# A third set for the accumulated weight sums in the up projection of a convolutional FFN, with the first sum's loads placed sooner and cache copies placed later

## The chip, the core and the metric

The kernel is one launch on one core of a Trainium2 chip. TensorE (PE) does the matrix products, VectorE (DVE) and ScalarE (ACT) elementwise work, GpSimd (POOL) small copies and those DMAs that add to what already stands at their destination, and SyncE (SP) issues most other DMAs. The metric is the device time in microseconds, median over runs.

## What is computed

One decoder layer over 512 prompt rows and 32 sample rows (8 sequences of 4 new tokens), all in float32: RMS norm, one input projection, retention and dilated attention, an output projection, and a feed-forward part with a causal convolution of width 3. The change lies in this last part and in the copying of the rolling key/value windows:

```python
def conv_ffn(h, conv_state, w_ffn_up, conv_w, conv_b, w_ffn_down):
    u = h @ w_ffn_up                       # (T, 1024) @ (1024, 2*2816)
    ext = jnp.concatenate([conv_state.astype(u.dtype), u], axis=1)
    c = conv_b + sum(conv_w[i] * ext[:, i:i + T] for i in range(CONV_W))
    g, val = c[..., :D_FF], c[..., D_FF:]
    f = (jax.nn.gelu(g, approximate=True) * val) @ w_ffn_down
    return f, ext[:, -(CONV_W - 1):]

# dilated_sample, for each of three groups of 128, 512 and 2048 cached rows:
new_buf = jnp.concatenate([buf, jnp.stack([k_new, v_new], axis=2)], axis=1)[:, -Wb:]
```

The new windows are the old ones moved by four rows, so almost all of each is a copy from one place in memory to another ("move" below, 511 KB for the large pieces). There are 88 moves: 44 are issued in the loop beside the input projections, 44 from the first up-projection loads on (iterator `moves`, L674).

## The kernel before

**Three passes for one product.** Every float32 product is done as three products of rounded halves: a weight tile is loaded raw, ACT makes its high part (a copy to fp32r), DVE the low part (raw minus high), and PE multiplies high by high, high by low and low by high.

**The up projection, in pairs.** The 5632 output columns are 22 pairs of tiles of 128 columns, a gate tile and a value tile (pair n, FT = 22). Pairs 0 to 2 (NPLAIN = 3) are plain: the two weight slots of a pair pass through `wraw`, `whi`, `wlo` (L2133, `up_half`). Pairs 3 to 21 are done by a scheme that needs seven half-size products instead of eight, on sums and differences of weight quarters and of operand quarters. Six of the seven are made in three passes (`three_passes`, L2185: 12 matmuls of 128 x 272), product 4 in one plain float32 pass (L2245, 8 matmul rows). PE's order is that of `up_products` (L87): for pair n products 6, 5, 7, then product 1 of pair n + 1, then 4 and 3 of pair n, then product 2 of pair n + 1 (L2256 to L2265). The semaphore `product` counts them; other engines and the queues wait for its values.

**The weight sums.** For pair n the tile `s13_raw` must hold the two quarters of the value weights' low half plus a quarter of the gate weights and of the value weights. It is filled in two steps: SP loads the value's low half twice side by side (`load_v_low`, L686, one DMA of 512 KB), and when that has landed POOL issues a DMA that adds 512 KB of gate and value weights to it in place (`add_to_v_low`, L959). Then ACT makes the high part (`sums_13_hi`, L1461), DVE adds `v_high` for the second sum (`sum_2`, L2844) and makes the low part over the raw tile (`sums_13_lo`, L2862, `s13_low` has the place of `s13_raw`). There are two sets of it, by n - 3 modulo 2 (`pair_set`). The tile of pair n is last read by product 7 of pair n, so SP issues the load for pair n + 2 after product 7 of pair n (L711).

**Queues of the engines.** Each engine works in program order. ACT does, in pair n: first_tap(n - 1), `keep_second(n)` (the result of product 6), **`sums_13_hi(n + 1)`**, `keep_third(n)` (the result of product 7, L1494), gelu(n - 1), `gate_hi(n + 2)` (L1451, high part of the gate weights of pair n + 2), `keep_first(n + 1)`, `sums_24_hi(n + 1)`, value_first(n), first_tap(n) (L1547 to L1570). Product 4 of pair n waits for `keep_third(n)` (r_neg, L2243), product 6 of pair n + 1 for the low part of the second sums (s24_lo, L2216). DVE's order is at L2927 to L2950. SP does in pair n: wait for product 2, `load_g(n + 2)`; wait for product 7, `load_v_low(n + 2)`, one move; wait for product 4, `load_v_high(n + 2)`, one move (L707 to L716). POOL does conv_heads(n + 2), add_to_v_low(n + 2), conv_tails(n).

**The first summed pair.** SP loads the last four plain slots with a move behind each (L695), and then those of pair 3 (L699 to L702). The set 1 tile of pair 4 lies over `whi`, so it can be loaded only when the plain pairs are done (w_used, L705).

**The down projection.** 22 slots of 512 KB through `wraw` (L722). SP puts one move behind each load until there are none left, which is the case after six. Near its end POOL reads back the residual rows (L987).

Of the kernel before, what the change touches and what calls it, by code (L numbers as in the profile page):

```python
# [44 lines left out]
TILES = 5  # L45
# [215 lines left out]
def build_layer(nc, a, o):  # L261
# [259 lines left out]
    g_in, vl_in, vh_in, sum_in = ([sem(f"{nm_}{e}") for e in range(2)] for nm_ in ("g_in", "vl_in", "vh_in", "sum_in"))  # L521
# [4 lines left out]
    x2_saved, x2_back = sem("x2_saved"), sem("x2_back")  # L526
# [61 lines left out]
    def set_count(n):  # L588

        return 16 * ((n - NPLAIN) // 2 + 1)  # L590

# [29 lines left out]
    def _(sp):  # L621
# [85 lines left out]
        for n in range(NPLAIN, FT - 2):  # L707
# [4 lines left out]
            load_v_low(n + 2)  # L712
            move(*next(moves))
# [33 lines left out]
    def _(pool):  # L747
# [182 lines left out]
        for p, i in enumerate(NORM_ORDER):  # L930
            pool.wait_ge(x2_ready, 2 * p + 2)
            pool.dma_start(x2_dram[i, 0:rows(i), :], xo[0:rows(i), i, :]).then_inc(x2_saved, 16)
# [52 lines left out]
        pool.dma_start(gfin[:], a["norm_ffn_post"].broadcast_to([128, D])).then_inc(gfin_in, 16)  # L985
        for i in range(TILES):
            pool.dma_start(xo[0:rows(i), i, :], x2_dram[i, 0:rows(i), :]).then_inc(x2_back, 16)  # L987
# [8 lines left out]
    def _(act):  # L996
# [7 lines left out]
        def w_split(s):  # L1004
# [456 lines left out]
        def sums_13_hi(n):  # L1461

            e = pair_set(n)
            act.wait_ge(sum_in[e], set_count(n))
# [4 lines left out]
            nc.scalar.activation(s13_high[e][:], s13_raw[e][:], ACT.Copy).then_inc(s13_hi, 1)  # L1469
# [122 lines left out]
    def _(pe):  # L1592
# [592 lines left out]
        def three_passes(b, fresh, Wh, Wl, w0, Th, Tl):  # L2185

            for k in range(4):
                cut = slice(w0 + 128 * k, w0 + 128 * k + 128)
                mm(b[:, 0:HALF], Wh[:, cut], Th(k), start=fresh and k == 0, stop=False, skip_group_check=not fresh)  # L2189
                mm(b[:, 0:HALF], Wh[:, cut], Tl(k), start=False, stop=False, skip_group_check=not fresh)  # L2190
                last = mm(b[:, 0:HALF], Wl[:, cut], Th(k), start=False, stop=k == 3, skip_group_check=not fresh)  # L2191
# [862 lines left out]
```

## Time and profile before

| | before |
|---|---|
| median of 3 runs (lowest to highest) | 1034.82 us (1033.66 to 1035.28) |
| profiled execution: time, span of its trace | 1034.72 us, 1032.9 us |
| PE busy (matmul) | 978.5 us, 95% |
| DVE, ACT, POOL busy | 600.7, 424.8, 230.7 us (58%, 41%, 22%) |
| DMA queue of SP, DMA queue of POOL | 130.76 MB, 63.07 MB |
| pair 3, product 4 starts; pair 20, product 4 starts | 649.20 us, 871.77 us |

The profile is one execution with the time of every instruction on each engine. The span begins with the first instruction; the profiled execution's own time is 1.8 us more than its span, and 0.1 us under the median of the three runs. PE is busy nearly all the time on average, but an average over the whole span hides the one stretch, the summed pairs from 635 to 885 us, in which it isn't. "idle ... <- X" behind a row means that the engine stood still before it, and that X ended the wait. A PE row's duration includes what it spends in the pipeline behind its neighbours, so the rate of PE is read from start to start.

### The profile page before, as it was taken

The page shows a single profiled execution, that of the slowest core. Times are in us where ns is not written, and L with a number is a line of the kernel's source. Part 1 is how long each engine was busy: PE and PEld are TensorE (multiplying, and loading weights), DVE is VectorE, ACT ScalarE, POOL GpSimd, SP SyncE. Part 2 cuts the span into 40 slices and gives each one's busy share as a digit, 9 for nine tenths or more (in the row PEclk, how much of TensorE's full clock was granted, in tenths as well). Part 3 has the DMA queues.
Part 4 walks back from the last instruction along what each step waited for, and adds up shares of the span by engine and source line. Part 5 has one row for each costly group of instructions (what it writes and reads, how often), then busy time and mean ns, then how long its engine had stood idle before and what let it go on. Part 6 is the DMA issues. An engine that isn't in the chain of part 4 may idle for free. (4 is left out here: it accounts for less than half of the span.)

```text
span 1032.9 us, 19094 instructions
## 1 busy us (share of the span) xinstructions
PE 978.5 (95%) x7470; PEld 858.5 (83%) x7470; DVE 600.7 (58%) x1029; ACT 424.8 (41%) x851; POOL 230.7 (22%) x394
## 2 busy tenths in 40 slices
PE   5999999999999999999999998889988899999997
PEld 4788778779999999998887797888988888777775
DVE  5255125534458876872165896677876677743135
ACT  5233232442453333322234654455554554633413
POOL 2102004134252434445010002222222221000200
PEclk9999999999999999999999999999999999999999
DMA  6644545547687676679453455777877776242723
GB/s 236 232 155 160 179 151 182 178 158 243 240 285 233 208 220 211 202 237 318 150 169 102 148 187 133 204 204 208 246 203 218 215 216 181 94 146 83 218 83 115
DMA packets 52070, 195.02 MB, mean 189 GB/s; under 512 B 7704, under 2 KB 8152, under 8 KB 50448
## 3 DMA queue, kind: packets, MB, share of 16 engines
q1 hardware_dynamic: 30784, 130.76, 37.2%
q0 software_dynamic: 21200, 63.07, 21.8%
q8 instruction: 59, 0.97, 0.4%
q14 instruction: 27, 0.22, 0.1%
HBM read 181.57 MB, written 56.27 MB: 230 GB/s over the span
## 5 line engine op out<-in xcount | busy, mean ns | idle before, releaser
L2309 DVE TENSOR_TENSOR wlo<-wraw,whi 128x1024 fp32r<-128x1024 f32 x94 | 114.9, 1222 | 265.1 <-ACT whi L1021 264.9
L1021 ACT ACTIVATE whi<-wraw 128x1024 fp32r<-128x1024 f32 x96 | 101.6, 1060 | 307.0 <-PE bank L1625 183.1
L1623 PE MATMUL bank<-whi,T1h 128*128 128x512 f32 (+1 forms) x288 | 114.5, 397 | 0.5 <-POOL wlo L762 0.3
L1705 PE MATMUL bank<-T1h,whi 128*128 128x272 f32 x384 | 113.4, 295 | 0.0
L1711 PE MATMUL bank<-T1h,wlo 128*128 128x272 f32 x384 | 111.0, 289 | 0.0
L1624 PE MATMUL bank<-wlo,T1h 128*128 128x512 f32 (+1 forms) x288 | 110.8, 385 | 0.0
L1625 PE MATMUL bank<-whi,T1l 128*128 128x512 f32 (+1 forms) x288 | 110.8, 385 | 0.0
L1710 PE MATMUL bank<-T1l,whi 128*128 128x272 f32 x384 | 110.4, 287 | 0.0
L1705 PEld LDWEIGHTS bank<-T1h,whi 128*128 128x128 f32 x384 | 72.3, 188 | 4.8 <-issue 4.5
L1710 PEld LDWEIGHTS bank<-T1l,whi 128*128 128x128 f32 x384 | 72.4, 189 | 0.0
L1711 PEld LDWEIGHTS bank<-T1h,wlo 128*128 128x128 f32 x384 | 72.2, 188 | 0.0
L1623 PE MATMUL bank<-whi,fTh 128*128 128x512 f32 x176 | 71.4, 406 | 0.0
L2245 PE MATMUL bank<-t4raw,v_high 128*128 128x272 f32 x152 | 45.5, 450 | 26.1 <-ACT rr L1498 26.1
L1624 PE MATMUL bank<-wlo,fTh 128*128 128x512 f32 x176 | 69.5, 395 | 0.0
L1623 PEld LDWEIGHTS bank<-whi,T1h 128*128 128x128 f32 x288 | 58.5, 203 | 13.1 <-issue 3.5
L1625 PE MATMUL bank<-whi,fTl 128*128 128x512 f32 x176 | 69.4, 394 | 0.0
L1625 PEld LDWEIGHTS bank<-whi,T1l 128*128 128x128 f32 x288 | 58.7, 204 | 10.0
L1624 PEld LDWEIGHTS bank<-wlo,T1h 128*128 128x128 f32 x288 | 58.8, 204 | 8.8
L2245 PEld LDWEIGHTS bank<-t4raw,v_high 128*128 128x128 f32 x152 | 31.2, 214 | 34.2 <-issue 28.0
L964 POOL DMA_DIRECT2D s_raw<-in_weights x19 | 22.7, 1196 | 121.0 <-DMA s_raw<-in_weights 113.6
L2494 DVE TENSOR_TENSOR prod<-kvk,qbc 128x512 f32<-128x512 f32 x48 | 33.0, 688 | 25.2 <-DMA qbc<-sample_queries 24.3
L1438 ACT ACTIVATE c<-u,convp 128x560 f32<-128x560 f32 x44 | 37.4, 856 | 20.3 <-DVE u L2888 19.6
(363 smaller groups left out, 2572.6 us busy)
## 6 DMA issues: line engine op xcount, KB each, us to landing
wraw<-in_weights SPq DMA_DIRECT2D x104, 512.0 KB, 4.4
out_s_kv_g<-in_cache_kv_g SPq DMA_DIRECT2D x64, 511.0 KB
qbc<-sample_queries POOLq DMA_DIRECT2D x48, 256.0 KB, 5.1
s_raw<-in_weights SPq DMA_DIRECT2D x19, 512.0 KB, 4.8
g_raw<-in_weights SPq DMA_DIRECT2D x19, 512.0 KB, 6.4
s_raw<-in_weights POOLq DMA_DIRECT2D x19, 512.0 KB, 7.2
kvk<-in_cache_kv_g POOLq DMA_DIRECT2D x32, 256.0 KB, 3.8
kvv<-in_cache_kv_g POOLq DMA_DIRECT2D x16, 512.0 KB, 8.2
```

Of the source, the lines that this page charges most:

```text
L964: pool.dma_start(s13_raw[e][:].rearrange("p (a c) -> p a c", a=2), src, accum_op=ALU.add).then_inc(sum_in[e], 16)
L1021: nc.scalar.activation(w_halves(s)[0], wraw[:, s % 2, :], ACT.Copy).then_inc(w_hi, 1)
L1438: nc.scalar.activation(cbs[:, n % 2, j, :], ubs[:, n % 3, j, 2:UW], ACT.Identity, scale=convp[:, tile, 2:3], bias=convp[:, tile, 3:4]).the ...
L1623: one = mm(P[i][:, 0:w], xh, Wh, start=st, stop=False)
L1624: mm(P[i][:, 0:w], xh, Wl, start=False, stop=False)
L1625: return one, mm(P[i][:, 0:w], xl, Wh, start=False, stop=sp_)
L1705: one = mm(dst, Wh, Th[:, k, c], start=k == 0, stop=False)
L1710: mm(dst, Wh, Tl[:, k, c], start=False, stop=False)
L1711: last = mm(dst, Wl, Th[:, k, c], start=False, stop=k == kt - 1)
L2245: last = mm(P[bank_a(n)][:, 0:HALF], v_high[e][:, 128 * k:128 * k + 128], t4raw[:, k, :], start=False, stop=k == 3, skip_group_check=True)
L2309: v.tensor_tensor(lo, wraw[:, s % 2, :], hi.bitcast(F), ALU.subtract).then_inc(w_lo, 1)
L2494: step(v.tensor_tensor(prod[:].rearrange("p (t n) -> p t n", t=2), keys, qbc[n % 3][:], ALU.mult))
```

## The change

It does five things.

1. A third set of `s13_raw`/`s13_low`, in columns of `T1h` that are no longer read once the plain pairs are done. The set of pair n is n - 3 modulo 3 (`sum_set`). Because the free columns are rows of 256 with gaps, the tile is now seen as 4 x 256 throughout. The high part keeps two sets.
2. SP now issues the low value half of pair n + 3 after product 7 of pair n, and POOL the adding DMA for pair n + 3. The load of pair 5 stands directly behind that of pair 4.
3. Each of the two DMAs is issued as two of 256 KB; a sum is complete after both.
4. The loads of pair 3 stand ahead of the last two plain slots and of the moves.
5. One move in each summed pair instead of two, and 25 moves instead of 6 in the down projection (one behind even slots, two behind odd ones). The read-back of the residual rows uses the same semaphore as their saving.

```diff
-    s13_raw = [sb(f"s13_raw{e}", S13_AT[e], [128, SLOT]) for e in range(2)]
-    s13_low = [sb(f"s13_low{e}", S13_AT[e], [128, SLOT], R) for e in range(2)]
-    s13_high = [sb(f"s13_high{e}", S13H_AT[e], [128, SLOT], R) for e in range(2)]
+    s13_raw = [sb(f"s13_raw{e}", S13_AT[e], [128, 4, 256]) for e in range(2)]
+    s13_low = [sb(f"s13_low{e}", S13_AT[e], [128, 4, 256], R) for e in range(2)]
+    s13_raw.append(sb("s13_raw2", 0, [128, 4, NTOK])[:, :, HALF:HALF + 256])
+    s13_low.append(sb("s13_low2", 0, [128, 4, NTOK], R)[:, :, HALF:HALF + 256])
+    s13_high = [sb(f"s13_high{e}", S13H_AT[e], [128, 4, 256], R) for e in range(2)]
...
+    def sum_set(n):
+        return (n - NPLAIN) % 3
+    def sum_count(n):
+        return 16 * ((n - NPLAIN) // 3 + 1)
...
         def load_v_low(n):
-            src = w_dram[S_UP + 2 * n + 1][:, 512:SLOT].unsqueeze(1).broadcast_to([128, 2, 512])
-            sp.dma_start(s13_raw[pair_set(n)][:].rearrange("p (a c) -> p a c", a=2), src).then_inc(vl_in[pair_set(n)], 16)
+            r = sum_set(n)
+            src = w_dram[S_UP + 2 * n + 1][:, 512:SLOT].rearrange("p (c w) -> p c w", c=2)
+            for a_ in range(2):
+                sp.dma_start(s13_raw[r][:, 2 * a_:2 * a_ + 2, :], src).then_inc(vl_in[r], 16)
...
-        for s in range(S_UP + 2, S_UP + 2 * NPLAIN):
+        for s in range(S_UP + 2, S_UP + 4):
             load_one(s)
-            move(*next(moves))
         sp.wait_ge(w_used, S_UP)
         load_v_low(NPLAIN)
+        load_v_high(NPLAIN)
         load_g(NPLAIN)
-        load_v_high(NPLAIN)
         load_v_high(NPLAIN + 1)
+        for s in range(S_UP + 4, S_UP + 2 * NPLAIN):
+            move(*next(moves))
+            load_one(s)
         sp.wait_ge(w_lo, S_UP + 2 * NPLAIN)
         load_g(NPLAIN + 1)
         sp.wait_ge(w_used, S_UP + 2 * NPLAIN)
         load_v_low(NPLAIN + 1)
+        load_v_low(NPLAIN + 2)
         for n in range(NPLAIN, FT - 2):
...
             sp.wait_ge(product, PRODUCT_NO[n, 7])
-            load_v_low(n + 2)
-            move(*next(moves))
+            if n + 3 < FT:
+                load_v_low(n + 3)
...
-            for m in itertools.islice(moves, 1):
+            for m in itertools.islice(moves, 2 if s % 2 else 1):
...
         def add_to_v_low(n):
-            e = pair_set(n)
-            pool.wait_ge(vl_in[e], set_count(n))
-            src = w_dram[S_UP + 2 * n:S_UP + 2 * n + 2].rearrange("s p (h c) -> p h s c", h=2)[:, 0]
-            pool.dma_start(s13_raw[e][:].rearrange("p (a c) -> p a c", a=2), src, accum_op=ALU.add).then_inc(sum_in[e], 16)
+            r = sum_set(n)
+            pool.wait_ge(vl_in[r], 2 * sum_count(n))
+            for a_ in range(2):
+                src = w_dram[S_UP + 2 * n + a_][:, 0:512].rearrange("p (c w) -> p c w", c=2)
+                pool.dma_start(s13_raw[r][:, 2 * a_:2 * a_ + 2, :], src, accum_op=ALU.add).then_inc(sum_in[r], 16)
...
+            if n == NPLAIN:
+                add_to_v_low(NPLAIN + 1)
+                add_to_v_low(NPLAIN + 2)
             if n >= 1 and n + 2 < FT:
                 conv_heads(n + 2)
-            if n == NPLAIN - 1:
-                add_to_v_low(NPLAIN + 1)
-            if NPLAIN <= n < FT - 2:
-                add_to_v_low(n + 2)
+            if NPLAIN <= n < FT - 3:
+                add_to_v_low(n + 3)
             conv_tails(n)
```

SP's queue around the first summed pairs, before. `wraw` are the last plain slots, `out_s_kv` a move, `s13_raw`, `g_raw` and `v_high` the loads of summed pairs (0 and 1 the set):

```order
L680 DMA wraw_52<-in_weights 128x1024
L654 DMA out_s_kv_g2<-in_cache_kv_g2 16x8176
L680 DMA wraw_52<-in_weights 128x1024
L654 DMA out_s_kv_g2<-in_cache_kv_g2 16x8176
L689 DMA s13_raw0_195<-in_weights 128x2x512
L684 DMA g_raw0_189<-in_weights 128x1024
L693 DMA v_high0_207<-in_weights 128x512
L693 DMA v_high1_208<-in_weights 128x512
L684 DMA g_raw1_190<-in_weights 128x1024
L689 DMA s13_raw1_196<-in_weights 128x2x512
L684 DMA g_raw0_189<-in_weights 128x1024
L689 DMA s13_raw0_195<-in_weights 128x2x512
```

The same place now:

```order
L691 DMA wraw_52<-in_weights 128x1024 x2
L702 DMA s13_raw0_195<-in_weights 128x512 x2
L706 DMA v_high0_209<-in_weights 128x512
L695 DMA g_raw0_189<-in_weights 128x1024
L706 DMA v_high1_210<-in_weights 128x512
L665 DMA out_s_kv_g2<-in_cache_kv_g2 16x8176
L691 DMA wraw_52<-in_weights 128x1024
L665 DMA out_s_kv_g2<-in_cache_kv_g2 16x8176
L691 DMA wraw_52<-in_weights 128x1024
L695 DMA g_raw1_190<-in_weights 128x1024
L702 DMA s13_raw1_196<-in_weights 128x512 x2
L702 DMA s13_raw2_199<-in_weights 128x2x256 x2
```

Pair 3's loads stand two slots and two moves sooner, pair 5's directly behind pair 4's, and the third set's rows are 256 long where those of the other sets are 512.

POOL's queue about pairs 3 to 5, before (`u<-cv_state` are conv_heads, `cv_tail<-u` conv_tails):

```order
L946 COPY u_149<-cv_state_155 128x8x2 x2
L964 DMA s13_raw1_196<-in_weights 128x2x512
L955 COPY cv_tail_154<-u_149 128x2
L956 COPY cv_tail_154<-u_149 128x16
```

and now:

```order
L971 COPY cv_tail_154<-u_149 128x2
L972 COPY cv_tail_154<-u_149 128x16
L981 DMA s13_raw1_196<-in_weights 128x512 x2
L981 DMA s13_raw2_199<-in_weights 128x2x256 x2
L962 COPY u_149<-cv_state_155 128x8x2 x2
L981 DMA s13_raw0_195<-in_weights 128x512 x2
```

The adding DMA of pair 4 has gone behind the tails of pair 2, with pair 5's directly behind it, ahead of the heads of pair 5.

## Rows read from the trace of the kernel before

**Rows 1.** Waits of PE, whole span: who waited for whom, us, times, longest.

```profile
PE bank L2245 <- ACT rr L1498: 26.1, 10, 3.9
PE bank L2189 <- ACT s L1486: 3.5, 1, 3.5
PE bank L2143 <- DVE wlo L2309: 1.8, 2, 1.4
```

**Rows 2.** Stretches between product 4 of pairs: length, busy times, granted clock, DMA share, GB/s.

```profile
649.20:664.15 14.95, 11.03 (x83) 10.52 (x81) 8.19 (x13) 5.82 (x10) 3.19 (x7) 1.00 0.86 263
664.15:676.71 12.56, 12.56 (x81) 12.02 (x81) 11.01 (x19) 7.37 (x12) 4.51 (x7) 0.86 0.57 149
691.25:702.23 10.98, 10.98 (x81) 10.67 (x81) 10.88 (x19) 7.36 (x12) 4.49 (x7) 1.00 0.66 172
...
860.82:871.77 10.95, 10.95 (x81) 10.64 (x81) 10.85 (x19) 7.01 (x11) 3.05 (x5) 1.00 0.74 216
649.20:871.77 222.57, 197.06 (x1363) 187.56 (x1361) 162.81 (x256) 112.08 (x170) 56.89 (x117) 0.95 0.78 220
```

**Rows 3.** Timeline of SP, POOL, ACT and PE, pair 4: start, duration, instruction.

```profile
647.88 0.38 SPq L689 DMA_DIRECT2D s_raw<-in_weights  x1
653.15 1.18 POOL L964 DMA_DIRECT2D s_raw<-in_weights  x1 [6.78 <-DMA s_raw<-in_weights]
662.66 1.06 ACT L1469 ACTIVATE s_high<-s_raw 128x1024 fp32r<-128x1024 f32 x1 [6.50 <-DMA s_raw<-in_weights]
663.62 0.38 ACT L1498 ACTIVATE rr<-bank 128x272 f32<-128x272 f32 x1
664.15 0.47 PE L2245 MATMUL bank<-t4raw,v_high 128*128 128x272 f32 x1 [3.92 <-ACT rr L1498]
```

**Rows 4.** Timeline of SP, ACT, DVE and PE in a pair without a wait.

```profile
696.37 0.33 SPq L684 DMA_DIRECT2D g_raw<-in_weights  x1
701.77 1.05 ACT L1459 ACTIVATE g_high<-g_raw 128x1024 fp32r<-128x1024 f32 x1
704.32 1.22 DVE L2873 TENSOR_TENSOR s_low<-s_raw,s_high 128x1024 fp32r<-128x1024 f32 x1
707.09 0.29 PE L2189 MATMUL bank<-t2hi,s_high 128*128 128x272 f32 x1
```

**Rows 5.** The tile g_raw, all its loads: issue to landing.

```profile
DMA to landing us min/median/max: 3.5/6.4/8.2
```

**Rows 6.** Timeline of ACT, DVE, SP and PE at the first summed pair.

```profile
593.10 0.35 SPq L680 DMA_DIRECT2D wraw<-in_weights  x1
...
621.93 1.07 ACT L1021 ACTIVATE whi<-wraw 128x1024 fp32r<-128x1024 f32 x1
626.82 0.69 DVE L2853 TENSOR_TENSOR s_raw<-s_raw,v_high 128x512 f32<-128x512 f32 x1 [6.03 <-DMA s_raw<-in_weights]
627.43 1.22 DVE L2309 TENSOR_TENSOR wlo<-wraw,whi 128x1024 fp32r<-128x1024 f32 x1
635.04 0.38 SPq L689 DMA_DIRECT2D s_raw<-in_weights  x1
637.94 0.67 ACT L1444 ACTIVATE c<-c 128x560 f32<-128x560 f32 x1 [6.40 <-DVE c L2780]
641.55 0.51 PE L2189 MATMUL bank<-t2hi,s_high 128*128 128x272 f32 x1 [3.52 <-ACT s L1486]
645.20 1.06 ACT L1469 ACTIVATE s_high<-s_raw 128x1024 fp32r<-128x1024 f32 x1 [0.20 <-DMA s_raw<-in_weights]
```

**Rows 7.** Timeline of SP and ACT in the down projection.

```profile
889.39 0.53 SPq L680 DMA_DIRECT2D wraw<-in_weights  x1
899.90 1.06 ACT L1021 ACTIVATE whi<-wraw 128x1024 fp32r<-128x1024 f32 x1 [3.55 <-PE bank L1625]
980.62 1.06 ACT L1021 ACTIVATE whi<-wraw 128x1024 fp32r<-128x1024 f32 x1 [8.01 <-DMA wraw<-in_weights]
983.91 1.06 ACT L1021 ACTIVATE whi<-wraw 128x1024 fp32r<-128x1024 f32 x1 [2.23 <-PE bank L1625]
```

More of the change, by code:

```diff
@@ L520, in build_layer @@
     product = sem("product")
-    g_in, vl_in, vh_in, sum_in = ([sem(f"{nm_}{e}") for e in range(2)] for nm_ in ("g_in", "vl_in", "vh_in", "sum_in"))
+    g_in, vh_in = ([sem(f"{nm_}{e}") for e in range(2)] for nm_ in ("g_in", "vh_in"))
+    vl_in, sum_in = ([sem(f"{nm_}{e}") for e in range(3)] for nm_ in ("vl_in", "sum_in"))
     g_hi, g_lo, s13_hi, s13_lo, s24_made, s24_hi, s24_lo = (
@@ L525, in build_layer @@
     s1_ready, q_ready, r_neg = sem("s1_ready"), sem("q_ready"), sem("r_neg")
-    x2_saved, x2_back = sem("x2_saved"), sem("x2_back")
+    x2_moved = sem("x2_moved")
     gelu_done, f_done, f_hi, f_lo = sem("gelu_done"), sem("f_done"), sem("f_hi"), sem("f_lo")
@@ L931, in _ @@
             pool.wait_ge(x2_ready, 2 * p + 2)
-            pool.dma_start(x2_dram[i, 0:rows(i), :], xo[0:rows(i), i, :]).then_inc(x2_saved, 16)
+            pool.dma_start(x2_dram[i, 0:rows(i), :], xo[0:rows(i), i, :]).then_inc(x2_moved, 16)
         pool.wait_ge(w_used, S_UP)
@@ L985, in _ @@
         pool.dma_start(gfin[:], a["norm_ffn_post"].broadcast_to([128, D])).then_inc(gfin_in, 16)
+        pool.wait_ge(x2_moved, 16 * TILES)
         for i in range(TILES):
-            pool.dma_start(xo[0:rows(i), i, :], x2_dram[i, 0:rows(i), :]).then_inc(x2_back, 16)
+            pool.dma_start(xo[0:rows(i), i, :], x2_dram[i, 0:rows(i), :]).then_inc(x2_moved, 16)
         pool.wait_ge(state_out_done, 16)
@@ L1016, in w_split @@
                 act.wait_ge(product, PRODUCT_NO[FT - 2, 7])
+                assert sum_set(FT - 3) == 1
             elif s == S_DN + 1:
@@ L1463, in sums_13_hi @@
             e = pair_set(n)
-            act.wait_ge(sum_in[e], set_count(n))
+            act.wait_ge(sum_in[sum_set(n)], 2 * sum_count(n))
             if n >= NPLAIN + 2:
@@ L1468, in sums_13_hi @@
                 act.wait_ge(w_used, S_UP + 2 * NPLAIN)
-            nc.scalar.activation(s13_high[e][:], s13_raw[e][:], ACT.Copy).then_inc(s13_hi, 1)
+            nc.scalar.activation(s13_high[e][:], s13_raw[sum_set(n)][:], ACT.Copy).then_inc(s13_hi, 1)
         def sums_24_hi(n):
@@ L2188, in three_passes, with sums_13 @@
                 cut = slice(w0 + 128 * k, w0 + 128 * k + 128)
-                mm(b[:, 0:HALF], Wh[:, cut], Th(k), start=fresh and k == 0, stop=False, skip_group_check=not fresh)
-                mm(b[:, 0:HALF], Wh[:, cut], Tl(k), start=False, stop=False, skip_group_check=not fresh)
-                last = mm(b[:, 0:HALF], Wl[:, cut], Th(k), start=False, stop=k == 3, skip_group_check=not fresh)
+                wh, wl = (Wh[k], Wl[k]) if isinstance(Wh, list) else (Wh[:, cut], Wl[:, cut])
+                mm(b[:, 0:HALF], wh, Th(k), start=fresh and k == 0, stop=False, skip_group_check=not fresh)
+                mm(b[:, 0:HALF], wh, Tl(k), start=False, stop=False, skip_group_check=not fresh)
+                last = mm(b[:, 0:HALF], wl, Th(k), start=False, stop=k == 3, skip_group_check=not fresh)
             last.then_inc(product, 1)
         first_half, second_half = slice(0, HALF), slice(HALF, NTOK)
+        def sums_13(n, half):
+            return [[t[:, 2 * half + k // 2, 128 * (k % 2):128 * (k % 2) + 128] for k in range(4)]
+                    for t in (s13_high[pair_set(n)], s13_low[sum_set(n)])]
         def product_1(n):
@@ L2229, in product_5 @@
                 pe.wait_ge(u_two[1], NPLAIN)
-            three_passes(P[bank_c(n)], True, s13_high[e], s13_low[e], 512, lambda k: t1hi[:, k, :], lambda k: t1lo[:, k, :])
+            three_passes(P[bank_c(n)], True, *sums_13(n, 1), 0, lambda k: t1hi[:, k, :], lambda k: t1lo[:, k, :])
         def product_7(n):
@@ L2235, in product_7 @@
             pe.wait_ge(q_ready, pair_no(n))
-            three_passes(P[bank_a(n)], False, s13_high[e], s13_low[e], 0, lambda k: t3hi[:, k, :], lambda k: t3lo[:, k, :])
+            three_passes(P[bank_a(n)], False, *sums_13(n, 0), 0, lambda k: t3hi[:, k, :], lambda k: t3lo[:, k, :])
         def product_4(n):
@@ L2792, in f_product @@
             if n >= 13:
-                dve.wait_ge(x2_saved, 16 * TILES)
+                dve.wait_ge(x2_moved, 16 * TILES)
             dve.wait_ge(gelu_done, n + 1)
@@ L2846, in sum_2 @@
             e = pair_set(n)
-            dve.wait_ge(sum_in[e], set_count(n))
+            r = sum_set(n)
+            dve.wait_ge(sum_in[r], 2 * sum_count(n))
             dve.wait_ge(vh_in[e], set_count(n))
@@ L2852, in sum_2 @@
                 dve.wait_ge(w_used, S_UP + 2 * NPLAIN)
-            v.tensor_tensor(s24_raw[e][:, 0:512], s13_raw[e][:, 0:512], v_high[e][:], ALU.add).then_inc(s24_made, 1)
+            v.tensor_tensor(s24_raw[e][:, 0:512].rearrange("p (c w) -> p c w", c=2), s13_raw[r][:, 0:2, :],
+                            v_high[e][:].rearrange("p (c w) -> p c w", c=2), ALU.add).then_inc(s24_made, 1)
         def sum_4(n):
@@ L2866, in sums_13_lo @@
             dve.wait_ge(s24_made, 2 * pair_no(n) - 1)
-            v.tensor_tensor(s13_low[e][:], s13_raw[e][:], s13_high[e][:].bitcast(F), ALU.subtract).then_inc(s13_lo, 1)
+            r = sum_set(n)
+            v.tensor_tensor(s13_low[r][:], s13_raw[r][:], s13_high[e][:].bitcast(F), ALU.subtract).then_inc(s13_lo, 1)
         def sums_24_lo(n):
@@ L2976, in _ @@
                 step(v.tensor_tensor(fo[0:rows(i), i, 0:512], fo[0:rows(i), i, 0:512], gfin[0:rows(i), 0:512], ALU.mult))
-        dve.wait_ge(x2_back, 16 * TILES)
+        dve.wait_ge(x2_moved, 32 * TILES)
         for p, i in enumerate(LAST_ORDER):
```

## The prediction

> **What bounds the kernel now.** I read the waits of PE first, since PE is busy 95% of the span. Three kinds of wait stand there that touch this change: 26.1 us in ten waits of product 4 for ACT's `rr` (`keep_third`), 3.5 us once for ACT's `s` (`keep_first`), and up to 1.4 us once for a low weight part [rows 1]. All lie in the up projection, so I cut that into stretches from one product 4 to the next. A pair without a wait takes 10.95 to 10.98 us; a pair with one takes about 15, and the next, which has no wait at all, takes 12.56 at a mean granted clock of 0.86 [rows 2]. The clock has two levels, 1.2 and 2.4 GHz; 0.86 means that part of that pair ran at the lower one, after PE had stood still. So a wait is paid twice, once as idle time and once as about 12.56 - 10.95 = 1.6 us of slower products. 17 periods took 222.57 us; at 10.95 they would take 186.15. These 36.4 us are what is to be had there.
>
> The timeline of pair 4 shows who is late [rows 3]. SP issues the low value half of pair 5 at 647.88, right after product 7 of pair 3. POOL waits until it has landed and issues the adding DMA at 653.15. ACT waits for that until 662.66, 14.8 us after the first issue. `keep_third(4)` is queued behind it on ACT, and product 4 starts 1.49 us after the sum came, having waited 3.92 us. Without that wait the sum would have had to be there at about 662.66 - 3.92 = 658.7, 10.9 us after the first issue. The chain of two DMAs is 3.9 us too long for the one period that two sets leave it.
>
> **Third set, steady state.** A sum now has one more period: 10.9 + 10.95 = 21.8 us. The chain needs 14.8, plus 0.38 for the second load issue and 1.18 for the second adding issue, 16.4; 5.4 us are left. So the wait goes away unless the chain grows by more than a third. The split into halves and the third set's rows of 256 are in no row. From below they cost nothing, or gain a little, since the first half can start before the second is issued. From above the two adding DMAs run one after the other, each as long as one now (662.66 - 653.15 = 9.5 us): 9.5 more, which is 4.1 beyond the spare. I take 1.6, near the lower end, since the bytes are the same and the issue time is the nearest row.
>
> Do the DMAs as a whole fit? Now the 17 periods move 220 GB/s x 13.09 us = 2.88 MB each. One move of 0.51 MB leaves: 2.37 MB, in 10.95 us 216 GB/s. That is the rate of the last period in rows 2, which had no wait, at a DMA share of 0.74. Yes.
>
> What is late next? The gate weights. Their load is issued after product 2, ACT comes to them 5.4 us later, and the low part of the second sums, which product 6 waits for, is done at 705.54 with product 6 at 707.09 [rows 4]: 1.55 us spare. A gate load may take 5.4 + 1.55 = 6.95 us for nothing. Now they take 6.4 in the median and 8.2 at most [rows 5], with two moves ahead of them in SP's queue where there will be one. I expect few waits, of tenths. `v_high` and `sum_4` have the place they had; POOL's second issue of 1.18 us is ahead of its tail copies, for which nobody waits before three pairs later.
>
> Sum for the 16 periods from product 4 of pair 4 (664.15) to that of pair 20 (871.77): 207.62 - 16 x 10.95 = **32.4 us**.
>
> **The start.** Pair 3's loads now go out right after the load at 593.10; needed is the sum by 620.8 (626.82 less DVE's idle 6.03) [rows 6]. That is 27 us for a chain of 15, even if POOL comes to it ten later. Then DVE makes the last plain low part when ACT's high part is ready, 621.93 + 1.07 = 623.0, instead of at 627.43: 4.4 us sooner. PE's wait of 1.4 us at the last plain slot goes. DVE works without a pause from 627.43 to the end that ACT's gelu at 637.94 waits for, and from there 3.6 us lead to product 6 of pair 3; so product 6 starts at 641.55 - 4.4 = 637.1.
>
> But pair 4's set lies over `whi`, and its load still waits for the plain pairs. It moves only with PE, from 635.04 to 633.6. Load to sum took 645.20 - 635.04 = 10.2, so the sum comes at 643.8 and product 4 of pair 3 at 643.8 + 1.49 = 645.3. PE alone would be there at 637.1 + four products. A period without a wait is 10.95, of which from product 4 to product 6 are 707.09 - 702.23 = 4.86, so four products are 6.1: 643.2. Here **a new wait of 2.1 us** takes the place of the 3.5. Before, product 4 stood at 649.20: 3.9 us sooner. Whether 2.1 us of standing still lowers the clock I bound by 10.95 and 12.56 for the next period and take the second, as after the wait of 3.9: product 4 of pair 4 at 657.9 instead of 664.15, **6.3 us** sooner. Bounds: without the new wait and its slow stretch 10.0; with both halves paid in full, 1.6 us later, 4.7.
>
> A rule speaks against the split here. The Trainium skill ("DMA: Bandwidth & Descriptors", section "Anatomy of one DMA") gives each DMA a fixed cost of about 2 us beside its bytes. If the halves came one after the other, load and add would each grow by 2 us. In steady state 16.4 would become about 19 and fit still; at the start product 4 of pair 3 would come 4 us later and the time would be 4 us more. No row here shows two adding DMAs back to back.
>
> **The end of the up projection.** The last period has a wait of 0.6 that comes from product 7 directly, with no product 1 between. It stays.
>
> **Down projection.** 25 moves instead of 6. Loads come in twos, each two slots apart; the second stands behind one move, as now, and its slot is wanted 10.5 us after its issue (889.39 to 899.90, where ACT waits for PE) [rows 7]. The added moves stand behind the second load, where nothing follows for many us. One place is tight: beside the read-back of the residual rows ACT waited 8.01 us for a weight load until 980.62. High and low part are made by 982.9, and PE frees the next slot at 983.9: 1.0 us spare. I allow **1.0 us** for this place and stray waits for gate loads together. The changed semaphore of the read-back costs nothing; all its saves are over long before.
>
> **Sum.** 6.3 + 32.4 - 1.0 = 37.7 us. From the profiled execution's 1034.72 that gives 997.0; the median shown is 0.1 more, so **997 us**. Its own range: with no new wait at the start and no allowance 42.4 less, 992.3; with the start at its lower bound (1.6 more) and 0.2 us more in each of 17 periods (3.4), 1002.
>
> **Rivals.**
>
> *Gate loads bind.* Landing at 7.5 instead of 6.4 costs 0.55 us a period, at 8.2 1.25: 9 to 21 us for 17 periods, 1006 to 1018. For it: loads that take over 6.95 exist now, and the adding DMAs lie beside them in every period. Against: one move fewer ahead, and the last period of rows 2 had this rate. Chance 0.15.
>
> *The halves are slow.* If they run partly one after the other, the chain grows by more than the 1.6 us taken. Up to the spare of 5.4 us that costs the start alone, us for us: 5 more give 1002. At the upper end of 9.5, 4.1 us are late in each of the 16 periods, 66 us, and the gain is gone; I give that end 0.01 of this rival's chance, since the bytes are the same. Chance 0.10. By the rule of the Trainium skill above it would be 1001.
>
> *The third set doesn't remove the wait,* because the chain is long for want of DMA bandwidth: in the waiting period the share is 0.86 at 263 GB/s. Then only the start is gained: 1028. Against: the mean of 220 would carry 2.37 MB in 10.8 us. Chance 0.04.
>
> *Slower: the moves delay the down projection's weights.* Each move's packets stand ahead of what follows in SP's queue. From a landing later than 10.5 us after issue PE waits, once in each of ten twos, and everything above 3.8 us a time makes the kernel slower than before; landings of 15 us give 10 x 4.5 = 45 us more than the forecast, 1042. For it only the tight place at 980; against it the place of the moves in the queue. Chance 0.05.
>
> The forecast keeps 0.66. About 0.2%, 2 us, is what a measurement of this kernel tells from no change. Only the last rival is on the slower side: faster 0.94, same 0.01, slower 0.05. The range of 993 to 1007 leaves out the last two rivals, the worse half of the gate loads and a little below: 0.18.
>
> **What would show it.** Right: the ten waits of product 4 for `rr` are one, at pair 3, about 2 us, and the periods from pair 5 on take 11.0 us at a clock of 1.00. Product 6 of pair 3 starts 4.4 us sooner. ACT no longer waits for DMA ahead of `s13_high`. Wrong: waits of product 6 for the second sums with ACT standing before `g_high` (gate loads); adding DMAs that take over 15 us from POOL's first issue (halves); waits of PE between slots of the down projection (moves); a period stuck near 13 us (bandwidth).

## The result, and the profile after

The changed kernel takes 996.79 us in the median of 4 runs (995.04 to 1000.05), the kernel before 1034.24 us (1032.22 to 1035.28) beside it. The ratio is 0.9644, interval [0.9613, 0.9674]. The profiled execution of the changed kernel took 995.9 us, its span is 994.1 us.

The waits of PE, which were [rows 1] before; columns as there:

```profile
PE bank L2271 <- ACT rr L1518: 3.0, 2, 2.4
PE bank L2210 <- DVE s_low L2902: 1.0, 1, 1.0
PE bank L2210 <- ACT s L1506: 0.8, 1, 0.8
PE bank L1662 <- DMA wraw<-in_weights: 0.9, 1, 0.9
```

Of the ten waits of product 4 for `rr` (26.1 us) two are left. One is the wait of 0.6 us in the last pair, which was there before, the other the new one of 2.4 us in pair 3. The second and the fourth line are waits that the kernel before did not have.

The stretches between product 4 of pairs, as [rows 2]: pair 3 to 4 (the one at a lower clock), 4 to 5, 10 to 11 (the longest behind it, at full clock, with the wait of 1.0 us of product 6 in it), 19 to 20, and the 16 periods from pair 4 to pair 20.

```profile
643.43:655.91 12.48, 12.47 (x80) 11.70 (x81) 10.99 (x19) 7.12 (x11) 3.83 (x8) 0.88 0.75 190
655.91:666.98 11.07, 11.07 (x82) 10.60 (x81) 9.59 (x16) 6.61 (x10) 3.77 (x8) 1.00 0.78 218
...
721.52:733.66 12.14, 11.13 (x82) 10.60 (x81) 9.58 (x16) 6.95 (x11) 4.13 (x8) 1.00 0.79 206
821.07:831.95 10.88, 10.88 (x83) 10.56 (x82) 9.64 (x16) 6.59 (x10) 1.41 (x4) 1.00 0.50 174
655.91:831.95 176.04, 174.95 (x1283) 169.22 (x1282) 153.88 (x241) 105.67 (x160) 76.13 (x124) 1.00 0.81 211
```

The same 16 periods of the kernel before, for the comparison:

```profile
664.15:871.77 207.62, 186.03 (x1281) 177.04 (x1281) 154.63 (x244) 106.26 (x161) 53.70 (x110) 0.95 0.78 217
```

207.62 us have become 176.04, at a granted clock of 1.00 instead of 0.95. PE's busy time fell by 11.1 us without any change of its work: that is the part of the waits' price that was paid as slow products. The remaining 20.5 us were idle.

The start, as [rows 6] and [rows 3]: the timeline of SP, POOL, ACT and PE around the first summed pair.

```profile
634.72 0.36 PE L2210 MATMUL bank<-t2hi,s_high 128*128 128x272 f32 x1 [0.84 <-ACT s L1506]
635.05 1.74 POOL L981 DMA_DIRECT2D s_raw<-in_weights  x2 [1.93 <-DMA s_raw<-in_weights]
636.99 2.44 POOL L981 DMA_DIRECT2D s_raw<-in_weights  x2 [0.20 <-issue]
...
641.95 1.06 ACT L1489 ACTIVATE s_high<-s_raw 128x1024 fp32r<-128x1024 f32 x1 [5.06 <-DMA s_raw<-in_weights]
642.91 0.38 ACT L1518 ACTIVATE rr<-bank 128x272 f32<-128x272 f32 x1
643.43 3.60 PE L2271 MATMUL bank<-t4raw,v_high 128*128 128x272 f32 x8 [2.43 <-ACT rr L1518]
```

Product 6 of pair 3 (first line) waits 0.84 us where it waited 3.5; then product 4 waits for `rr`, which stands on ACT behind the high part of pair 4's sum, and that for its adding DMA.

To compare executions I count from one instruction that all kernels have at the end of the part before the change, DVE's first `t3raw`. It starts at 608.79 us before and at 606.35 us after:

```profile
608.79 1.28 DVE L2816 TENSOR_TENSOR t3raw<-x_sum 128x1088 f32<-128x1088 f32 x1
```

```profile
606.35 1.28 DVE L2842 TENSOR_TENSOR t3raw<-x_sum 128x1088 f32<-128x1088 f32 x1
```

Over the profiles of this study it lies between 604.2 and 609.0 us, in no order that follows the edits. So the 2.4 of the 38.8 us between the two spans that lie before it are taken as variation between executions. The table has all profiles, in us from `t3raw`; P6(3) is the start of product 6 of pair 3, "rest" the time from P4(20) to the last matmul.

| kernel | P6(3) | P4(3) | P4(4) | P4(20) | rest | median of all its runs |
|---|---|---|---|---|---|---|
| before | 32.8 | 40.4 | 55.4 | 263.0 | 155.2 | 1034.2 |
| changed | 28.4 | 37.1 | 49.6 | 225.6 | 156.2 | 996.8 |
| changed, measured again later | 28.4 | 37.1 | 48.1 | 223.3 | 156.6 | 994.6 |
| third set alone | 32.2 | 39.8 | 50.7 | 227.2 | 155.2 | 997.1 |
| third set undone | 28.4 | 35.9 | 47.1 | 244.6 | 157.0 | 1014.6 |
| ... and whole DMAs | 28.4 | 36.2 | 48.6 | 244.7 | 156.5 | 1019.0 |
| ... and two moves a pair | 28.4 | 36.4 | 49.7 | 246.6 | 155.2 | 1023.4 |
| early loads alone | 28.4 | 36.5 | 49.1 | 259.7 | 155.2 | 1031.2 |
| old order of loads | 32.5 | 40.2 | 51.0 | 226.4 | 156.1 | 998.5 |
| whole DMAs | 28.4 | 37.9 | 48.8 | 225.5 | 156.5 | 998.2 |
| two moves a pair | 28.4 | 36.8 | 47.8 | 223.7 | 155.2 | 997.5 |
| pair 3 reordered | 28.4 | 34.5 | 45.8 | 220.4 | 157.0 | 992.6 |
| no moves at the tight slots | 28.4 | 37.2 | 49.6 | 224.7 | 155.2 | 996.0 |
| pair 3 reordered, two moves a pair | 28.4 | 34.5 | 45.4 | 221.8 | 155.1 | 991.5 |

The account of the two profiled executions: 2.4 us before `t3raw`, 5.8 by P4(4), 31.6 in the 16 periods, less 1.0 in the rest. That makes 38.8.

### The profile page after: what moved, and what is told of

Read it like the earlier page. It is cut to its first block, busy times and chain, and to the rows that moved or that the text cites. A ratio compares the mean times of both kernels' runs of the same rounds, so it can differ in the third digit from the quotient of the medians.

```text
span 994.1 us, 19133 instructions
## 1 busy us (share of the span) xinstructions
PE 965.1 (97%) x7470; PEld 848.6 (85%) x7470; DVE 601.7 (61%) x1029; ACT 424.4 (43%) x851; POOL 268.3 (27%) x413
## 4 chain that ended last, share of the span: by engine, by line
PE 85%; DMA 5%; DVE 5%; ACT 2%; issue 1%; POOL 0%; SPq 0%; DVEq 0%; ACTq 0%
PE bank L1643 11%; PE bank L1645 10%; PE bank L1644 10%; PE bank L1725 6%; PE bank L1731 6%; PE bank L1730 6%; PE bank L2210 5%; PE bank L2212 5%; PE bank L2211 5%; PE bank L2271 3%; PE bank L1662 3%; PE bank L1625 2%; DMA wraw<-in_weights 2%; DMA g_raw<-in_weights 2%; PE bank L2060 1%
## 5 line engine op out<-in xcount | busy, mean ns | idle before, releaser
L981 POOL DMA_DIRECT2D s_raw<-in_weights x38 | 37.5, 1171 | 81.1 <-DMA s_raw<-in_weights 80.9
L962 POOL COPY u<-cv_state 128x16 f32<-128x16 f32 x44 | 41.8, 1047 | 35.5 <-DVE c L2806 31.0
L2520 DVE TENSOR_TENSOR prod<-kvk,qbc 128x512 f32<-128x512 f32 x48 | 33.0, 687 | 22.8 <-DMA qbc<-sample_queries 21.8
L2212 PE MATMUL bank<-T1h,g_low 128*128 128x272 f32 x152 | 44.0, 290 | 0.0
L2210 PE MATMUL bank<-T1h,g_high 128*128 128x272 f32 x152 | 43.9, 289 | 0.0
```

What stands on the lines that cost most here:

```text
L962: nc.gpsimd.tensor_copy(u_samples(n, j)[:, :, 0:2], cvs[:, 16 * tile:16 * tile + 16].rearrange("p (b t) -> p b t", t=2)).then_inc(head_rea ...
L2210: mm(b[:, 0:HALF], wh, Th(k), start=fresh and k == 0, stop=False, skip_group_check=not fresh)
L2212: last = mm(b[:, 0:HALF], wl, Th(k), start=False, stop=k == 3, skip_group_check=not fresh)
```

## The experiments

Each undoes or does one part. Ratios are to the kernel before, measured again beside each run on the same chip.

**Third set undone.** The set of a sum and its count go back from thirds to halves, and load and adding DMA to pair n+2:

```
-        return (n - NPLAIN) % 3
+        return (n - NPLAIN) % 2
...
-            if n + 3 < FT:
-                load_v_low(n + 3)
+            load_v_low(n + 2)
```

> The changed kernel with the third buffer alone undone: sums alternate between two sets again, the value load for pair n+2 and its adding DMA stand at pair n; halves, early loads of pair 3 and the shifted moves stay. Theory A (the third set carries the steady gain): the chain of load and add has one period again. In the changed kernel a load behind product 7 lands after 3.0 to 3.6 us and its add's second half 7.9 to 9.3 us after the issue, 12 to 13.5 us together against the 10.9 us that one period allows, so product 4 waits for rr 1 to 2.5 us in most of the 17 pairs, with slow stretches behind some: 997 + 17 x (1 to 2.5), 1012 to 1035, I take 1022. Rival B (one move fewer per pair and the halves carry it, the third set little): the chain fits by itself, at most 3 waits of product 4, 995 to 1003.

1014.55 us, ratio 0.9801 [0.9769, 0.9834]. The waits for `rr` are back:

```profile
PE bank L2267 <- ACT rr L1514: 19.4, 12, 2.8
```

Its 16 periods from pair 4 to pair 20, columns as in [rows 2]:

```profile
652.07:849.56 197.49, 179.94 (x1280) 172.56 (x1281) 153.90 (x244) 106.19 (x161) 63.94 (x126) 0.98 0.72 193
```

Theory A holds, B falls. But beside the other edits the third set is worth 18 us by the medians and 21.5 in the 16 periods (197.5 to 176.0), and not 32: with two sets the other edits have taken 10.1 of the 207.6 us away. The timeline shows the chain as it now is in one pair, SP, POOL, ACT and PE:

```profile
673.46 0.80 SPq L702 DMA_DIRECT2D s_raw<-in_weights  x2
677.77 1.78 POOL L979 DMA_DIRECT2D s_raw<-in_weights  x2 [5.27 <-DMA s_raw<-in_weights]
687.83 1.06 ACT L1485 ACTIVATE s_high<-s_raw 128x1024 fp32r<-128x1024 f32 x1 [5.41 <-DMA s_raw<-in_weights]
688.79 0.38 ACT L1514 ACTIVATE rr<-bank 128x272 f32<-128x272 f32 x1
689.31 2.74 PE L2267 MATMUL bank<-t4raw,v_high 128*128 128x272 f32 x8 [2.79 <-ACT rr L1514]
```

687.83 - 673.46 = 14.4 us in this pair. Others are shorter, the one before it 12.2 us; the twelve waits are 1.6 us each in the mean, the ten before were 2.6. So the time lies at the low end of what A expected.

**Two moves a pair.** One move more behind each value load, and one less behind every second load of the down projection:

```
             if n + 3 < FT:
                 load_v_low(n + 3)
+            move(*next(moves))
...
-            for m in itertools.islice(moves, 2 if s % 2 else 1):
+            for m in itertools.islice(moves, 1):
```

> The changed kernel with two moves in each pair again (as before) and one behind each load of the down projection. Theory A (the third set has 5 us to spare): 0.51 MB more in each of 14 pairs raises the demand to 2.88 MB in 10.95 us, 263 GB/s, which the trace of before shows for a whole waiting pair; product 4 does not wait, the gate loads land about 1 us later (7.5 to 9 us after issue) and product 6 waits for s_low some 0.5 to 1 us in most pairs: 1003 to 1012, I take 1006. Rival B (bandwidth was the bound): the chain grows past 16 us, product 4 waits for rr in most pairs, 1020 or more. Rival C (the shift does nothing): 996 to 998.

997.46 us, ratio 0.9640 [0.9615, 0.9665]: the time of the whole change. Rival C holds; my own expectation of 1006 falls. Its 16 periods, and the landing of its gate loads:

```profile
651.99:827.93 175.94, 175.31 (x1282) 169.34 (x1281) 153.91 (x241) 105.59 (x160) 86.78 (x124) 1.00 0.93 256
```

```profile
DMA to landing us min/median/max: 3.6/6.9/7.7
```

The DMA engines move 256 GB/s at a share of 0.93, and product 6 waits for the second sums twice, 0.6 us in all. The gate loads land at 6.9 us in the median, just below the 6.95 that the prediction had worked out as free. This profiled execution took 990.9 us, the lowest of the five runs and 6.6 under their median, so its row of the table says nothing on whether two moves are faster.

**Old order of the loads of pair 3.** All plain loads before the first value load, as before the change:

```
-        for s in range(S_UP + 2, S_UP + 4):
+        for s in range(S_UP + 2, S_UP + 2 * NPLAIN):
             load_one(s)
+            move(*next(moves))
         sp.wait_ge(w_used, S_UP)
         load_v_low(NPLAIN)
...
-        for s in range(S_UP + 4, S_UP + 2 * NPLAIN):
-            move(*next(moves))
-            load_one(s)
```

> The changed kernel with SP's order of the loads of pair 3 as before: all four plain weight loads, each with a move, then the value load of pair 3. Theory A: the low part of the last plain slot is made 4.4 us later again, product 6 of pair 3 starts 4.4 us later, the new wait of 2.4 us at product 4 of pair 3 shrinks by what comes later, and the rest of the up projection is shifted by 4 to 6 us; one move more stands before the up projection and one less in the down projection. 1000 to 1003, I take 1002. Rival (the start gained nothing by itself, since the load of pair 4 waits for the plain pairs anyway): 996 to 998.

998.52 us, ratio 0.9642 [0.9615, 0.9668]. By the trace P6(3) is 4.2 us later than in the changed kernel, near the 4.4 expected, but P4(4) only 1.5 and P4(20) 0.8 us. Product 4 of pair 3 does not wait here, and no slow stretch follows:

```profile
648.46:659.33 10.87, 10.87 (x82) 10.55 (x81) 9.52 (x16) 6.25 (x10) 5.53 (x8) 1.00 0.79 207
659.33:834.65 175.32, 175.24 (x1283) 169.31 (x1281) 153.59 (x241) 105.72 (x160) 84.85 (x124) 1.00 0.83 212
```

The truth lies between the two. With the third set there, the early loads buy 0.8 us by P4(20), or 3.1 against the changed kernel's second profile, which had no slow stretch. Of the 4.2 us at P6(3) 3.1 are left at P4(3), behind the new wait, and the slow stretch behind it, where there is one, takes about 1.5 more.

**Whole DMAs.** Value load and adding DMA of sets 0 and 1 in one piece; set 2 keeps its halves, since its rows lie apart:

```
...
+            if r < 2:
...
+                pool.dma_start(s13_raw[r].rearrange("p (a c) w -> p a (c w)", a=2), src, accum_op=ALU.add).then_inc(sum_in[r], 16)
+            for a_ in range(2 if r == 2 else 0):
```

> The changed kernel with the value load and the adding DMA of sets 0 and 1 in one DMA each again; set 2 keeps its halves. Theory A (halves cost nothing, issue time 0.54 us twice against 1.18 us once): within 1 us of the changed kernel, 996 to 998; the chain of a whole sum as before, 14 to 15 us, is hidden in steady state by the third set, and only pair 4's sum at the start shows it: product 4 of pair 3 starts 0 to 1 us later. Rival B (halves add a fixed cost each): the whole DMAs end 2 to 4 us sooner, product 4 of pair 3 does not wait any more: 993 to 994.

998.24 us, ratio 0.9643 [0.9617, 0.9670]. Theory A holds, rival B falls: product 4 of pair 3 starts 0.8 us later with whole DMAs, not sooner. The changed kernel and three other profiles with halves and the same order on ACT have it within 36.8 to 37.2 us, so the 0.8 us are clear of what executions differ by.

**Pair 3 reordered.** In pair 3 alone ACT makes `rr` before the sum's high part, and DVE the value half and `f` before the sums of pair 4:

```
             keep_second(n)
-            if n + 1 < FT:
+            if NPLAIN < n < FT - 1:
                 sums_13_hi(n + 1)
...
                 keep_first(n + 1)
+                if n == NPLAIN:
+                    sums_13_hi(n + 1)
                 sums_24_hi(n + 1)
```

> The changed kernel with one pair in another order: in pair 3, ACT makes rr (keep_third) before the high part of pair 4's first sums instead of behind it, and DVE makes the value half, f, and then the sums of pair 4. Theory A (product 4 of pair 3 waits only because rr is queued behind the sum): product 4 of pair 3 starts 34.5 to 35 us after the first t3raw instead of 37.1, 2.4 us sooner, and product 6 of pair 4 waits at most 1 us for s_low; with or without a slow stretch behind, 993 to 995, I take 994. Rival (the wait only moves to product 6 or 5 of pair 4, which need the same sum): within 1 us of the changed kernel.

The changed kernel itself, beside it on the same chip:

> The changed kernel itself, for the comparison on this chip: 996 to 998.

992.60 us (990.57 to 993.60, 6 runs), ratio 0.9587 [0.9553, 0.9621]; the changed kernel there 994.56 us (994.15 to 998.68), ratio 0.9616 [0.9581, 0.9651]. The intervals overlap; the step is read from the trace, ACT, POOL, DVE and PE:

```profile
635.69 4.22 POOL L981 DMA_DIRECT2D s_raw<-in_weights  x4 [2.35 <-DMA s_raw<-in_weights]
639.76 0.40 ACT L1518 ACTIVATE rr<-bank 128x272 f32<-128x272 f32 x1 [2.63 <-PE bank L2214]
...
641.08 1.99 PE L2273 MATMUL bank<-t4raw,v_high 128*128 128x272 f32 x8
642.43 1.06 ACT L1489 ACTIVATE s_high<-s_raw 128x1024 fp32r<-128x1024 f32 x1 [0.48 <-DMA s_raw<-in_weights]
644.98 1.23 DVE L2904 TENSOR_TENSOR s_low<-s_raw,s_high 128x1024 fp32r<-128x1024 f32 x1
646.26 0.40 PE L2212 MATMUL bank<-t2hi,s_high 128*128 128x272 f32 x1 [0.17 <-DVE s_low L2904]
```

The sum lands as late as before (ACT comes to it at 642.43), but `rr` is no longer behind it. Product 4 of pair 3 does not wait, P4(3) comes at 34.5 instead of 37.1 us, and of the wait 0.2 us turn up at product 6 of pair 4. P4(20) is 2.9 us sooner than in the changed kernel beside it. Theory A holds for the trace; the median lies 2.0 us under the changed kernel's and 0.4 under the range that I gave.

**No moves at the tight slots** of the down projection (none behind the loads of slots 14 and 15, two behind 16 and 19):

> The changed kernel with no move behind the loads of slots 14 and 15 of the down projection, two instead of one behind slot 16 and two behind slot 19. Theory A (the moves in front of slot 16's load, beside the read-back of the residual, make the wait of 0.9 us): the wait goes, 1 us faster than the changed kernel, 995.5 to 996.5. Rival (the read-back alone delays it, as before the change, when the load was 8 us late for ACT without PE waiting): the wait stays, 996 to 998.

995.98 us, ratio 0.9619 [0.9585, 0.9653]. By time the 1 us that I expected isn't to be seen: the median is 1.4 us above the 994.56 of the changed kernel beside it, and the intervals overlap. In the trace no wait of PE for a weight load is left, and the rest is 155.2 us instead of 156.2 and 156.6. Theory A holds for the trace alone.

**Both together,** pair 3 reordered and two moves a pair:

> The order of pair 3 as in the kernel of that name, and in addition two moves in each pair and one behind each load of the down projection, as it was before the change: from the run with the moves back, no wait of PE in the down projection. Theory A (both gains add): 2.4 + 1.0 us or more below the changed kernel, 991.5 to 994, I take 993. Rival (gate loads behind the extra move make product 6 wait once pair 3 is no longer late): 995 to 997.

991.46 us (987.70 to 993.57), ratio 0.9571 [0.9535, 0.9607], the lowest median here, and a little under the changed kernel's 994.56. Against the reordering alone (992.60) it can't be told apart, and its interval overlaps the changed kernel's (0.9616 [0.9581, 0.9651]) too. In the traces P4(20) comes 1.4 us later than with the reordering alone, with waits of 1.1 us of product 6 for the second sums instead of 0.4, and the rest is 1.8 us shorter. So whether the two gains add (A) or the gate loads take one back (the rival) stays open.

**What took the 10 us with two sets.** Three kernels with two sets: whole DMAs, two moves a pair, and both, where only the early loads of the change are left.

> The run with two sets (1014.6) with each value load and each adding DMA in one piece again, and one move per pair as there. It splits the 10 us that the run with two sets gained between product 4 of pair 4 and of pair 20 (197.5 against 207.6 us before). Theory H (the halves shorten the chain, since POOL's issue is 0.54 us for the first half instead of 1.18 and half the bytes start sooner): the gain goes back, 204 to 208 us for the 16 periods, 1021 to 1026. Theory M (the move that left each pair's value load shortens it): it stays, 197 to 200 us, 1013 to 1017.

> The run with two sets, halves kept, and the second move back in each pair, ahead of the adding DMAs' packets. Theory H (halves shorten the chain): 16 periods in 197 to 200 us, 1013 to 1017. Theory M (the move does): 204 to 208 us, 1021 to 1026. With the run of whole DMAs this tells whether the two add.

> Of the change only SP's early loads of pair 3: two sets, whole DMAs, two moves in each pair. My step for the start gave it 6.3 us by product 4 of pair 4. Theory A (that step): product 6 of pair 3 4.4 us sooner, product 4 of pair 4 3 to 6 us sooner, the rest as before, 1029 to 1032. Rival B, by the run with the old order (where everything else made up for 3 of the 4.4 us): the sum of pair 4, whose load waits for the plain pairs, and two sets behind it hold product 4 of pairs 3 and 4 where they were; nothing is left: 1034 to 1036.

1019.00 us, ratio 0.9880 [0.9824, 0.9937]; 1023.44 us, ratio 0.9897 [0.9865, 0.9930]; 1031.23 us, ratio 0.9965 [0.9941, 0.9990]. For the early loads alone theory A holds, against rival B's 1034 to 1036: 1031.2 lies in its range, and P6(3) comes 4.4 us sooner. Their 16 periods took 196.1, 196.9 and 210.6 us. The last two in rows:

```profile
658.35:855.23 196.88, 179.23 (x1280) 171.34 (x1281) 152.20 (x241) 105.54 (x161) 65.86 (x126) 0.99 0.84 229
```

```profile
658.09:868.66 210.57, 186.47 (x1283) 176.72 (x1281) 151.66 (x238) 105.19 (x160) 51.41 (x110) 0.95 0.80 218
```

Neither H nor M is right as I put it: each edit alone brings the periods from 210.6 to about 196.5, and both together (197.5) bring no more in the trace. The times say otherwise. The profiled executions of these two were the fastest of their four and ten runs, so their traces flatter them: by the medians each edit alone takes 12.2 and 7.8 us off 1031.2, both together (1014.6) 16.7. The ratio of both together, 0.9801 [0.9769, 0.9834], is clear of that with halves and two moves, 0.9897 [0.9865, 0.9930], so beside the halves the move that is gone does count. Against whole DMAs with one move, 0.9880 [0.9824, 0.9937], the intervals overlap by a little, so what the halves bring beside one move stays open.

**The third set alone.** From the kernel before, only the third set, its own rows in halves. With it come what it needs, the loads and adding DMAs one pair further ahead with POOL's order at pairs 4 and 5, and the semaphore of the read-back:

> Of the change only the third set (its own rows of 256 in halves, since its tile has no other form), with whole DMAs in sets 0 and 1, two moves in each pair and SP's old order at pair 3. Theory A (the third set by itself takes all the waits): 16 periods in 175 to 177 us, product 4 of pair 4 51 us after the first t3raw, no wait in the down projection: 996 to 999, as the whole change. Rival B (whole DMAs and two moves bring gate loads or adds beyond the spare): 16 periods over 180 us, 1002 or more.

997.08 us, ratio 0.9642 [0.9605, 0.9678].

```profile
657.48:834.01 176.53, 175.51 (x1283) 169.32 (x1282) 153.54 (x241) 105.61 (x160) 83.53 (x114) 1.00 0.92 256
```

```profile
PE bank L2215 <- ACT s L1511: 3.5, 1, 3.5
PE bank L2168 <- DVE wlo L2340: 1.2, 2, 0.8
...
PE bank L2215 <- DVE s_low L2907: 1.0, 3, 0.6
```

At the start it waits the 3.5 us of the kernel before and 1.2 instead of 1.8 for low weight parts, but product 4 of pair 4 no longer waits; its 16 periods and its time those of the whole change. Theory A holds.

## Why the prediction was right

**Steady state: right.** Forecast 32.4 us, measured 31.6. The run with the third set alone shows that the set does it, and the run without it that the other edits together don't: as long as a sum has one period, a chain of 12 to 15 us is late. I had allowed the chain 16.4 us; in the profile of the changed kernel load and adding DMAs take 12.7 to 14.5 us together from pair 7 on, about as before (pair 6's take 17), so the halves lengthened nothing that can be seen. The missing 0.8 us is the wait of product 6 below, with what followed it.

**Bandwidth: right, for a stronger reason than given.** I argued from 2.37 MB in 10.95 us. The kernels with two moves move 256 GB/s, at 11.0 us a period (175.94 / 16). What the DMA engines can move was never the bound in these pairs; the time from issue to landing of two transfers in turn was. That time does hang on what else is in the queues: with two sets and whole DMAs one move fewer per pair shortened the 16 periods from 210.6 to 196.1 us, and 12.2 us by the medians.

**What is late next: right in place.** I expected few waits of product 6, of tenths. ACT now does wait for gate loads, 13 times, and one of these waits reaches PE, with 1.0 us:

```profile
  ACT g_high L1479: 17.0, 13
...
DMA to landing us min/median/max: 3.5/6.6/8.2
```

This is the tile `g_raw` in the changed kernel: 17.0 us in 13 waits of ACT, and landings as in [rows 5], not shorter for having one move fewer ahead. The one landing of 8.2 us is that of the load at 715.69. Its trail on SP, ACT, DVE and PE:

```profile
715.69 0.33 SPq L695 DMA_DIRECT2D g_raw<-in_weights  x1
723.93 1.06 ACT L1479 ACTIVATE g_high<-g_raw 128x1024 fp32r<-128x1024 f32 x1 [2.77 <-DMA g_raw<-in_weights]
726.26 1.23 DVE L2902 TENSOR_TENSOR s_low<-s_raw,s_high 128x1024 fp32r<-128x1024 f32 x1
727.54 0.39 PE L2210 MATMUL bank<-t2hi,s_high 128*128 128x272 f32 x1 [1.01 <-DVE s_low L2902]
```

8.2 - 6.95 = 1.25 us were to be expected by the working, and PE waited 1.01.

**The start: the size right, the cause half wrong.** Forecast 6.3 us by P4(4), measured 5.8. P6(3) came 4.4 us sooner, the new wait of product 4 was 2.4 us against 2.1, the next stretch 12.48 against 12.56. But I gave the 6.3 us to the early loads. The third set alone has 4.7 us by P4(4), because it takes the wait of 3.9 us there (the other 0.6 us are there already at P6(3)); the early loads alone have 6.3 as well (55.4 to 49.1), yet of these 3.3 are left at P4(20). Put together the two do not add, 4.7 and 6.3 make 5.8: they remove the same wait. What the early loads bring beside the third set is 0.8 to 3.1 us by the traces, and the medians of that chip (998.5 against 997.5 and 998.2) can't tell it from nothing.

**The slow stretch: in some executions, not in others.** I charged 1.6 us for it as certain. Five profiles have a wait of 2.1 to 3.2 us at P4(3). In the changed kernel and in that without moves at the tight slots the stretch behind it ran at 0.88; in the three others, one of them the changed kernel again, at 1.00:

```profile
643.65:656.07 12.42, 12.42 (x81) 11.64 (x82) 11.00 (x19) 7.13 (x11) 3.86 (x8) 0.88 0.76 196
```

```profile
643.74:654.70 10.96, 10.96 (x81) 10.65 (x81) 10.86 (x19) 7.02 (x11) 4.90 (x8) 1.00 0.79 195
```

```profile
646.46:657.41 10.95, 10.95 (x80) 10.64 (x81) 10.85 (x19) 7.02 (x11) 3.69 (x7) 1.00 0.81 200
```

The third, with whole DMAs, had the longest wait of all, 3.2 us, and no slow stretch. The early loads alone had a shorter one, 1.80 us, and behind it 12.62 us at a mean granted clock of 0.86. So the length of the wait doesn't tell which it will be. The slow stretch is 1.5 of the 2.3 us between the two profiles of the same changed kernel at P4(20).

**The halves: nothing.** The Trainium skill ("DMA: Bandwidth & Descriptors", section "Anatomy of one DMA") gives each DMA that GpSimd issues about 2 us of its own. I had added that to SP's load too, which the section doesn't speak of, and had let the halves follow one another, which made 4 us at product 4 of pair 3. The trace doesn't show it: that product started 0.8 us sooner with halves than with whole DMAs. The halves are in flight together. Of the two adding ones that POOL issues at 759.2 and 759.7 us the first lands 5.2 us after its issue and the second 7.2, which is 2.5 us behind the first. What part of a landing is a DMA's own cost was not measured. My bound for slow halves also counted the second issue twice: 14.8 + 0.4 + 9.5 = 24.7 us is 2.9 beyond the 21.8 that two periods give, not 4.1. Nothing else in the forecast hangs on that.

**The allowance of 1.0 us: right at the read-back, too small for both.** The timeline of POOL, SP, ACT and PE beside the read-back of the residual rows, as [rows 7]:

```profile
927.63 2.60 POOL L1006 DMA_DIRECT2D xo<-mid_rows  x5
...
933.51 1.14 SPq L665 DMA_DIRECT2D out_s_kv_g<-in_cache_kv_g  x2
934.75 0.53 SPq L691 DMA_DIRECT2D wraw<-in_weights  x1
...
945.45 1.06 ACT L1041 ACTIVATE whi<-wraw 128x1024 fp32r<-128x1024 f32 x1 [3.88 <-DMA wraw<-in_weights]
945.47 0.64 PE L1662 MATMUL bank<-wraw,fTs 128*32 128x128 f32 x16 [0.93 <-DMA wraw<-in_weights]
```

The load behind two moves landed 10.7 us after its issue, and PE waited 0.93 us. Without moves there the wait is gone. All seven profiles with the moves placed as in the change have it, with 0.8 to 1.6 us; none of the seven others has. The allowance was to cover stray waits for gate loads as well, and with the 1.01 us above these took 1.9 together. Elsewhere in the down projection the added moves cost PE no wait, so the rival on the slower side had its mechanism right at one place out of ten, at a price of 1 us.

**The sum.** 5.8 + 31.6 - 1.0 = 36.4 us explained, against 37.7 forecast; the medians differ by 37.5 us, and single executions of one kernel lie up to 5 us apart (995.0 to 1000.1). That forecast and median agree to 0.2 us is therefore luck; the mechanism of the 31.6 us is not.

So the third set alone gives the time of the whole change. Once it is there, splitting the DMAs brought nothing that can be measured, the early loads at most 3 us in the traces, and the shift of the moves costs the 1 us at the read-back.

## What to carry to other kernels

The wait on a chain of two transfers was removed here by giving the chain one more period, not by making the transfers cheaper: shortening it by two different means, alone or together, won 10 to 15 us of the 32 in the traces, and a third buffer all of it. When several edits aim at one wait, price them as alternatives and not as a sum, and ask which one alone is enough. If a buffer can't come sooner, look at what stands behind the waiting instruction on its engine: putting `rr` ahead of it in one pair made that wait vanish.

## What was not expected of the hardware

- Issuing the adding DMAs in halves takes POOL longer: 1.74 us for the two of set 1 and 2.44 for those of set 2, whose rows are of 256 elements, against 1.18 for the whole one [rows 3]. Of set 1's two the second is issued 0.5 us behind the first and takes 1.2 itself. POOL's busy time rose from 230.7 to 268.3 us. Nobody waits for it.
- Landing times of the adding DMAs follow their size only in part: in the kernel with the third set alone whole ones take 8.6 us in the median and set 2's halves, with half the bytes, 7.2. First the whole ones, then the halves:

```profile
DMA to landing us min/median/max: 5.9/8.6/9.6
...
DMA to landing us min/median/max: 6.0/7.2/8.6
```

- A DMA share of 0.92 to 0.93 in all of the 16 periods costs PE little: 1.0 us in three waits of product 6 with the third set alone, 0.6 in two with two moves a pair. The median landing of a gate load is 6.6 and 6.9 us there, against 6.6 in the changed kernel at 0.81.
- The same wait of PE (2.4 and 2.5 us in two executions of the changed kernel) is followed by a stretch at the lower clock in some executions and not in others of the same kernel, so one profile doesn't price it.
